# Two transformer blocks on one core: the first norm's gains, x and the first weights are loaded in another order and smaller pieces, and x is turned between the first products

## What is computed

```
h = rmsnorm(x, norm_mix_g[l])
proj = h @ w_in[l]            # (256, 2048) @ (2048, 4096)
```

## Time and profile before

| what | value |
|---|---|
| median of 3 runs | 2614.55 us (2613.58 to 2618.11) |
| the profiled execution, its own time | 2615.93 us |
| its span in the trace | 2613.8 us |
| TensorE busy in the span | 2590.8 us (99%) |
| VectorE, ScalarE busy | 1484.6 us (57%), 1105.7 us (42%) |
| first weight product starts | 13.41 us |
| granted clock of TensorE, mean | 0.996 of 2.4 GHz |

### The profile page before, as it was taken

How to read it: one execution, slowest core, us unless ns; L and a number is a source line. 1 busy time by engine, 2 the same in 40 slices (tenths; PEclk the granted TensorE clock), 3 DMA queues, 4 the chain that set the end, 5 groups by cost and what they waited for, 6 DMA issues and landing times.

```text
span 2613.8 us, 29869 instructions
## 1 busy us (share of the span) xinstructions
PE 2590.8 (99%) x13012; PEld 2188.5 (84%) x13012; DVE 1484.6 (57%) x1281; ACT 1105.7 (42%) x938; POOL 46.5 (2%) x58
## 2 busy tenths in 40 slices
PE   9999999999999999999999999999999999999998
PEld 7888888888888888888888887887888888888887
DVE  5465555544555455677678996534555544455444
ACT  5444454433444334455335444543354433344333
POOL 0000000000000000001001100000000000000000
PEclk9999999999999999999999999999999999999999
DMA  8544565666555655655334455553555555555553
GB/s 295 187 160 137 188 200 187 193 193 193 192 183 190 193 190 184 238 177 177 113 106 138 158 179 180 175 167 109 191 193 193 185 194 194 189 189 191 190 193 134
DMA packets 154753, 471.63 MB, mean 180 GB/s; under 512 B 7328, under 2 KB 7968, under 8 KB 153472
## 3 DMA queue, kind: packets, MB, share of 16 engines
q1 hardware_dynamic: 152208, 456.62, 53.2%
q0 software_dynamic: 1856, 11.54, 1.2%
q10 hardware_dynamic: 560, 1.57, 0.2%
HBM read 465.51 MB, written 4.19 MB: 180 GB/s over the span
## 4 chain that ended last, share of the span: by engine, by line
PE 96%; DVE 3%; ACT 1%; DMA 0%; issue 0%; POOLq 0%; SPq 0%; POOL 0%; ACTq 0%; DVEq 0%
PE ps L682 20%; PE ps L683 20%; PE ps L686 20%; PE ps L731 18%; PE ps L735 9%; PE ps L940 1%; DVE conv_out L1934 1%; PE ps L646 1%; PE ps L826 1%; DVE weights_lo L1714 1%; PE ps L1193 1%; PE ps L1209 1%; PE ps L1037 0%; PE ps L907 0%; PE ps L898 0%; PE ps L1111 0%
## 5 line engine op out<-in xcount | busy, mean ns | idle before, releaser
L1714 DVE TENSOR_TENSOR weights_lo<-weights_raw,weights_hi 128x2048 fp32r<-128x2048 f32 x431 | 986.8, 2290 | 926.8 <-ACT weights_hi L1277 926.8
L1277 ACT ACTIVATE weights_hi<-weights_raw 128x2048 fp32r<-128x2048 f32 x431 | 825.7, 1916 | 1149.1 <-PE ps L686 854.7
L682 PE MATMUL ps<-weights_hi,stationary 128*128 128x512 f32 x1408 | 559.3, 397 | 8.0 <-ACT stationary L1615 2.6
L683 PE MATMUL ps<-weights_lo,stationary 128*128 128x512 f32 x1408 | 549.9, 391 | 0.0
L731 PE MATMUL ps<-stationary,weights_hi 128*128 128x512 f32 x2048 | 547.9, 394 | 0.6 <-DVE residual L1747 0.6
L686 PE MATMUL ps<-weights_hi,stationary 128*128 128x512 f32 x1408 | 435.5, 391 | 0.0
L731 PEld LDWEIGHTS ps<-stationary,weights_hi 128*128 128x128 f32 x2048 | 354.6, 189 | 53.2 <-DVE residual L1747 0.9
L682 PE MATMUL ps<-weights_hi,hidden_hi 128*128 128x512 f32 x1016 | 395.3, 389 | 0.0
L683 PE MATMUL ps<-weights_lo,hidden_hi 128*128 128x512 f32 x1016 | 395.3, 389 | 0.0
L735 PEld LDWEIGHTS ps<-stationary,weights_lo 128*128 128x128 f32 x2048 | 305.5, 189 | 37.7
L682 PEld LDWEIGHTS ps<-weights_hi,stationary 128*128 128x128 f32 x1408 | 265.5, 189 | 65.0 <-issue 4.1
(11 more groups left out here) (320 smaller groups left out, 1106.9 us busy)
## 6 DMA issues: line engine op xcount, KB each, us to landing
weights_raw<-in_w SPq DMA_DIRECT2D x128, 1024.0 KB, 5.2
weights_raw<-in_w_in SPq DMA_DIRECT2D x79, 1024.0 KB, 5.2
weights_raw<-in_w_up SPq DMA_DIRECT2D x64, 1024.0 KB, 5.2
weights_raw<-in_w_down SPq DMA_DIRECT2D x64, 1024.0 KB, 5.4
weights_raw<-in_w_out SPq DMA_DIRECT2D x32, 1024.0 KB, 5.4
weights_raw<-in_wk SPq DMA_DIRECT2D x16, 1024.0 KB, 5.2
weights_raw<-in_wv SPq DMA_DIRECT2D x16, 1024.0 KB, 5.2
weights_raw<-in_wq SPq DMA_DIRECT2D x16, 1024.0 KB, 5.2
```

The source lines that it names most:

```text
L682: pe.matmul(o, xh, WHI[:, slot, j, c * BANK:(c + 1) * BANK], start=first and j == 0, stop=False)
L683: pe.matmul(o, xh, WLO[:, low, j, c * BANK:(c + 1) * BANK], start=False, stop=False)
L1277: act.activation(WHI[:, s % NSPLIT], RAW[:, s % NRAW], ACT.Copy).then_inc(hi_ready, 1)
L1714: dve.tensor_tensor(WLO[:, s % NRAW], RAW[:, s % NRAW], WHI[:, s % NSPLIT].bitcast(F32), ALU.subtract).then_inc(lo_ready, 1)
```

## The change

- `vectors` is loaded in two parts: the first block (64 KB, the gains of the norms) behind the identity, the other three (192 KB) behind weights 3. Both identity and gains count up `gains_landed`.
- `gains_turn` turns the one block; VectorE copies 128 columns and multiplies as before. The other three are turned by `vec_turn` ahead of step 6, into bank 7, and copied by VectorE after the low part of step 6. TensorE waits for this copy in the middle of step 7.
- x comes in pieces of tiles 0 and 1 (256 KB, ScalarE's queue), 2 and 3 (256 KB, between the halves of weights 0), 4 to 7 (512 KB, behind weights 1), and 8 to 15 (1024 KB, behind weights 2 and a wait of SyncE for the first piece).
- Ahead of step 0 only tiles 0 and 1 are turned and split, tiles 2 and 3 are turned after the first six products of step 0, and split behind the second half of weights 0. Two dummy products instead of four stand ahead of step 0.
- In steps 0 to 2 (`as_it_comes`) TensorE waits for each part just ahead of its first product, in the order high x high, low part of x x high, high part of x x low. The number of products is the same.

```
...
@@ -456,8 +456,8 @@
 
         @block.sync
         def _(sp):
-            sp.dma_start(VEC_RAW[:], vectors.rearrange("n r c -> r n c")).then_inc(vec_landed, 16)
-            sp.dma_start(SQ[:, 0, :], squares[:, 0, :]).then_inc(ident_landed, 16)
+            sp.dma_start(SQ[:, 0, :], squares[:, 0, :]).then_inc(gains_landed, 16)
+            sp.dma_start(VEC_RAW[:, 0, :], vectors[0]).then_inc(gains_landed, 16)
 
             def load(s, src):
 
@@ -469,9 +469,9 @@
                 for k in range(PS):
                     load(s0 + k, blocks(w)[(first + k) % PS, :, :, c0:c0 + COLS])
 
-            def load_x(n):
-                cols = slice(n * BANK, (n + 1) * BANK)
-                sp.dma_start(X[:, :, cols], x.rearrange("(t p) d -> p t d", p=P)[:, :, cols]).then_inc(x_landed[min(n, 2)], 16)
+            def load_x(n, first, end):
+                cols = slice(first * P, end * P)
+                sp.dma_start(X[:, :, cols], x.rearrange("(t p) d -> p t d", p=P)[:, :, cols]).then_inc(x_landed[n], 16)
 
             def load_up(s, src):
                 if s >= NRAW:
@@ -493,15 +493,19 @@
 
             first = blocks(w_in)[0, :, :, IN_COLS[0] * COLS:(IN_COLS[0] + 1) * COLS]
             sp.dma_start(RAW[:, 0, 0], first[:, 0]).then_inc(first_landed, 16)
+            load_x(1, 2, 4)
             sp.dma_start(RAW[:, 0, 1], first[:, 1]).then_inc(raw_landed[0], 16)
-            load_x(1)
             for n in range(4):
                 for k in range(PS):
                     if (n, k) != (0, 0):
                         load(S_IN + n * PS + k, blocks(w_in)[k, :, :, IN_COLS[n] * COLS:(IN_COLS[n] + 1) * COLS])
                     if (n, k) == (0, 1):
-                        load_x(2)
-                        load_x(3)
+                        load_x(2, 4, 8)
+                    elif (n, k) == (0, 2):
+                        sp.wait_ge(x_landed[0], 16)
+                        load_x(0, 8, KT)
+                    elif (n, k) == (0, 3):
+                        sp.dma_start(VEC_RAW[:, 1:, :], vectors[1:].rearrange("n r c -> r n c")).then_inc(vec_landed, 16)
                     elif (n, k) == (0, NRAW - 1):
                         sp.dma_start(SQ[:, 1:, :], squares[:, 1:, :]).then_inc(sq_landed, 16)
 
@@ -628,11 +632,14 @@
 
         @block.tensor
         def _(pe):
+            def gains_turn():
+                pe.wait_ge(gains_landed, 32)
+                pe.transpose(ps[:, 0, 0:P], VEC_RAW[:, 0, :], IDENT).then_inc(vec_turned, 1)
+
             def vec_turn():
                 pe.wait_ge(vec_landed, 16)
-                pe.wait_ge(ident_landed, 16)
-                for n in range(4):
-                    last = pe.transpose(ps[:, 0, n * P:(n + 1) * P], VEC_RAW[:, n, :], IDENT)
+                for n in range(1, 4):
+                    last = pe.transpose(ps[:, 7, n * P:(n + 1) * P], VEC_RAW[:, n, :], IDENT)
                 last.then_inc(vec_turned, 1)
 
             def turn8(src, half, group):
@@ -654,10 +661,7 @@
 
             def step(s, hi, lo, k, p, first, last, between=None):
 
-                if s == 0:
-                    pe.wait_ge(first_hi, 1)
-                    pe.wait_ge(first_lo, 1)
-                else:
+                if s >= NSPLIT:
                     pe.wait_ge(hi_ready, s + 1)
                     pe.wait_ge(lo_ready, s + 1)
                 slot, low, group = s % NSPLIT, s % NRAW, GROUPS[p]
@@ -671,10 +675,10 @@
                     if s == S_END - 1:
                         last_quarters(hi, lo, k, slot, low, group, t)
                         continue
+                    if s < NSPLIT:
+                        mm = as_it_comes(s, t)
+                        continue
                     for j in range(STEP):
-                        if (s, t, j) == (0, 0, 1):
-                            pe.wait_ge(hi_ready, 1)
-                            pe.wait_ge(lo_ready, 1)
                         xh = hi[:, k + j, t * P:(t + 1) * P]
                         xl = lo[:, k + j, t * P:(t + 1) * P]
                         for c in range(2):
@@ -689,6 +693,36 @@
                 if s < S_END - 1:
                     mm.then_inc(w_used, 1)
 
+            def as_it_comes(s, t):
+
+                for j in range(STEP):
+                    k = STEP * s + j
+                    xh = HHI[:, k, t * P:(t + 1) * P]
+                    xl = HLO[:, k, t * P:(t + 1) * P]
+                    if t == 0:
+                        pe.wait_ge(ht_hi, k + 1)
+                        if s == 0 and j == 0:
+                            pe.wait_ge(first_hi, 1)
+                        else:
+                            pe.wait_ge(hi_ready, s + 1)
+                    for c in range(2):
+                        pe.matmul(ps[:, 2 * t + c, :], xh, WHI[:, s, j, c * BANK:(c + 1) * BANK], start=k == 0, stop=False)
+                    if t == 0:
+                        pe.wait_ge(ht_lo, k + 1)
+                    for c in range(2):
+                        pe.matmul(ps[:, 2 * t + c, :], xl, WHI[:, s, j, c * BANK:(c + 1) * BANK], start=False, stop=False)
+                    if t == 0:
+                        if s == 0 and j == 0:
+                            pe.wait_ge(first_lo, 1)
+                        else:
+                            pe.wait_ge(lo_ready, s + 1)
+                    for c in range(2):
+                        mm = pe.matmul(ps[:, 2 * t + c, :], xh, WLO[:, s, j, c * BANK:(c + 1) * BANK], start=False, stop=False)
+                    if (s, t, j) == (0, 0, 0):
+                        pe.wait_ge(x_landed[1], 16)
+                        turn_tiles(residual, STEP, 2 * STEP, 1)
+                return mm
+
             def last_quarters(hi, lo, k, slot, low, group, t):
 
                 for c in range(2):
@@ -709,7 +743,7 @@
                         turn8(turn_second, 1, 1 - GROUPS[p])
                     if during:
                         during(k, 0)
-                    if h is not None:
+                    if h is not None and s0 + k >= NSPLIT:
                         stationary(h, STEP * (k + 1))
                     step(s0 + k, HHI, HLO, STEP * k, p, k == 0, k == PS - 1,
                          between=(lambda k=k: during(k, 1)) if during else None)
@@ -794,15 +828,20 @@
 
             pe.wait_ge(zeros_ready, 1)
             keep_busy(3)
-            vec_turn()
+            gains_turn()
             keep_busy(1)
 
             def during_wq_in(k, j):
                 if (k, j) == (1, 0):
-                    pe.wait_ge(x_landed[1], 16)
-                    turn_tiles(residual, 4, 8, 1)
+                    pe.wait_ge(x_landed[2], 16)
+                    turn_tiles(residual, 2 * STEP, 8, 1)
+                elif (k, j) == (6, 0):
+                    pe.wait_ge(ht_lo, KT * H_IN + KT)
+                    vec_turn()
+                elif (k, j) == (7, 1):
+                    pe.wait_ge(vec_ready, 2)
                 elif (k, j) == (2, 0):
-                    pe.wait_ge(x_landed[2], 32)
+                    pe.wait_ge(x_landed[0], 32)
                     pe.wait_ge(ht_lo, KT * H_IN + KT // 2)
                     turn8(residual, 1, 1)
 
@@ -814,9 +853,8 @@
                 pe.wait_ge(out1, p + 1)
 
             pe.wait_ge(x_landed[0], 16)
-            turn_tiles(residual, 0, 4, 1)
-            keep_busy(4)
-            pe.wait_ge(vec_ready, 1)
+            turn_tiles(residual, 0, STEP, 1)
+            keep_busy(2)
             gemm_pass(S_IN, P_IN, during_wq_in, H_IN)
 
             def turn_rows(src, group, done):
@@ -1363,25 +1401,26 @@
                     act.wait_ge(attended, h - 1)
                 act.activation(PT1[:, s, :], ps[:, 2 + s, 0:NS], ACT.Copy).then_inc(pt_ready, 1)
 
-            act.dma_start(X[:, :, 0:BANK], x.rearrange("(t p) d -> p t d", p=P)[:, :, 0:BANK]).then_inc(x_landed[0], 16)
+            act.dma_start(X[:, :, 0:T], x.rearrange("(t p) d -> p t d", p=P)[:, :, 0:T]).then_inc(x_landed[0], 16)
             act.wait_ge(halves_ready, 1)
             act.activation(table_warm[:], halves[:, 0:1], ACT.Copy)
             act.wait_ge(vec_ready, 1)
-            split_tiles(H_IN, lambda k: G_IN + k, 0, 4, 1)
+            split_tiles(H_IN, lambda k: G_IN + k, 0, STEP, 1)
             act.wait_ge(first_landed, 16)
             act.activation(WHI[:, 0, 0], RAW[:, 0, 0], ACT.Copy).then_inc(first_hi, 1)
             act.wait_ge(raw_landed[0], 16)
             act.activation(WHI[:, 0, 1], RAW[:, 0, 1], ACT.Copy).then_inc(hi_ready, 1)
+            split_tiles(H_IN, lambda k: G_IN + k, STEP, 2 * STEP, 1)
             for n in range(4):
                 for k in range(PS):
                     split_next(S_IN + n * PS + k)
                     if (n, k) == (0, 0):
-                        split_tiles(H_IN, lambda k: G_IN + k, 4, 8, 1)
+                        split_tiles(H_IN, lambda k: G_IN + k, 2 * STEP, 8, 1)
                     elif (n, k) == (0, 2):
                         split_turned(H_IN, lambda k: G_IN + k, 1, 1)
                     elif (n, k) == (0, 3):
```

(12 more changed lines are left out.)

2 lines of the change are left out of this document (1 added, 1 removed).

## The result

The changed kernel's median is 2611.64 us (20 runs, 2608.59 to 2614.69), that of the kernel before in the same comparison 2615.99 us (20 runs, 2612.76 to 2618.11). The medians are 4.35 us apart. Predicted were 2611.5 us in 2608.5 to 2615.0. In two later comparisons one run of the new version took 3914 and 4151 us, at a mean granted clock near 0.6, and is left out of the medians given for it.

A forecast was written before the change was run, and what follows sets the result against it. TensorE, busy 2590.8 of 2613.8 us, was taken as the bound, so only an earlier start helps: 4.5 us less 0.4, 0.44 and 0.33 is 3.3, taken as 3.0 for the clock; 2611.5 us predicted from 2614.55, range 2608.5 to 2615.0.

The forecast's parts named there:

- the working's 3.3: Whole start: 4.5 us gained at the first product, less 0.4, 0.44 and 0.33 us, gives 3.3 us.
- the clock term: Start: low clock from 8.0 to 11.4 us costs some 0.85 us, gain 2.45; otherwise 3.3; 3.0 taken.
- Transfers: First loads: 448 KB less ahead of the gains at 280 GB/s, 1.64 us; gains at 5.45, first half at 7.2 us.
- the first rival: Small pieces of x slow the queue: weights 1 at 14.2 us, gain 1.8 us, 2612.8 us; chance 0.17.
- From the gains to the first product: Start chain with two tiles on ScalarE and no wait for the low part: first product at 8.95 us, 4.5 gained.
- What goes back: Low part's wait 0.4 us, tiles 2 and 3 turned in step 0 0.44, step 6 transposes 0.33; second half nothing.
- the prediction's own early case: Gains at 4.0, first product at 7.5 us; second half holds tile 1; gain 4.1 us, 2610.5; chance 0.10.
- second way to step 1: Check on step 1's start: 20.00 us less 3.6 us gained is 16.4, against 16.1 by counting from step 0.
- The vectors' turn in step 6: VectorE waits for TensorE's step 6; low part of step 7 at 49.0, wanted at 51.2 us: costs nothing.
- First half not earlier: First half of weights 0 lands at 8.56 us as before: gain 2.5 us at full clock, 2612.3; chance 0.07.
- The slow case: Clock stays at 1.2 GHz while real products run; 2621 us at 20 us of it; chance 0.04, shared with one-by-one transfers.
- the gain at 27 us: Sign: products of step 2 at 23.4 to 24 us (27.22 before); prediction wrong if this gain isn't there at the end.

The follow-up runs named there:

- the four profiles: Profiles with the changed kernel's start as it is: its own two and those of experiment 8 and experiment 10; first pass taken out at 53.85 to 54.44 us.
- experiment 2: Changed kernel with tiles 0 to 3 of x in one piece again on ScalarE's queue: first pass taken out at 54.43 us, first product at 9.52.
- experiment 10: Wide sums and dummy products in the second block's waits, added to both kernels: 2611.41 us for the kernel before, 2607.62 us for the changed one.
- experiment 6: Changed kernel with one dummy product at the start and none of the three others: first pass taken out at 54.40 us (53.88 with the dummies).
- experiment 4: Kernel before with six more dummy products through TensorE's idle time from 4.1 to 7.2 us: first pass taken out at 56.60 us, 0.62 us less.
- experiment 8: Changed kernel with the layer norm's 16 sums of squares at 128 columns instead of 2: 2610.75 us, ratio to the kernel before 0.9983.

## Why the prediction was right

**The time.** 2611.5 predicted, 2611.64 measured. The mechanism is the predicted one, and the gain of 3.8 us without the spread (3.34 and 3.28 by the landmark in two pairs of profiles) stands beside the working's 3.3 and the chosen 3.0. The chosen value was low because of the clock term. That the times agree to 0.14 us is luck. The forecast took 3.05 us off a median of three runs, 2614.55; twenty runs have 2615.99, 1.4 us more, and the measured gain of 4.35 us is larger than the predicted one by 1.3. The two errors cancel, and both medians come from runs that spread over 5 to 6 us.

**Transfers.** The gains landed at 4.17 us (4.1 to 4.3 in the four profiles), near the lower bound of 4.0, not at 5.45. The rate of 280 GB/s, taken from the whole load, was the wrong measure for 128 KB at its very front. The first half came at 6.44 and not 7.2 in this execution, but at 7.8 and 7.5 in two others, so the 7.2 was fair. The other way, tiles 2 and 3 came at 8.3 (7.85 predicted), the second half at 9.51 (9.1; up to 10.2 in the four) and weights 1 at 12.1 (11.7): 0.4 us later than predicted, not the 2.5 of the first rival. Counted from the first half's landing in this execution it is 1.2 us. From 5 to 6.5 us the four profiles moved 168 to 213 GB/s, the three with the start of the kernel before 317 to 331, and experiment 2, with tiles 0 to 3 of x in one piece, 268. So the change's loads are slow there; which of its pieces makes it isn't shown.

**From the gains to the first product.** 8.11 us against 8.95, a gain of 5.3 us at this point and not 4.5. The copy of 128 columns took 0.29 us (0.28 assumed), and ScalarE's two tiles and half weights went as counted (1.93 us, 1.95 assumed). Of the 1.3 us by which the gains came earlier 0.45 were lost on the way to ScalarE's start, because the dummy product and the transposes of x weren't at full pace (4.22 to 6.18 us; in experiment 10 the same way took 1.31 us).

**What goes back.** The wait for the low part came, and was a little smaller: 1.17 us from the first product to the fifth, where the prediction had 1.25 (8.95 to 10.2). What it had wrong is the second half of weights 0, which it called free. Step 0's tile 1 begins at 10.74, 1.46 us after the fifth product and not 0.9, because TensorE waits for the high part; and tile 1 takes 4.52 us and not 4.1, because TensorE waits for the low part (11.90). Together that is 0.9 to 1.0 us. So step 0 took 7.15 us from its first product and not 6.25, which cancels the 0.8 us: two errors of one size, and that the sum came out is in part luck. It isn't luck alone, since the prediction's own early case says that the second half would hold tile 1 if the start came earlier. Step 0 ended at 15.26 us (15.2 predicted), step 1 began at 16.05 (16.1), and the turn ahead of step 2 at 21.59 (21.7), because from there on all goes by the tensor engine's own pace. This was the part to get right, and it was read from the engine's 46.6 us without idle time. For its second way to step 1 the prediction took 20.00 from the chain; the first product of step 1 is at 19.76 in the timeline of the kernel before, and 3.6 less is 16.2.

**The later steps.** The low part of weights 1 was ready at 16.34 and wanted at 17.0: cover of 0.7 us as predicted, no wait. The vectors' turn in step 6: VectorE waited 6.91 us, copied in 0.56, and had the low part of step 7 ready at 48.4, wanted at about 51; TensorE didn't wait:

```profile
45.68 0.56 DVE L1900 COPY vectors<-ps 128x384 f32<-128x384 f32 x1 [6.91 <-PE ps L642]
46.16 4.48 DVE L1753 TENSOR_TENSOR weights_lo<-weights_raw,weights_hi 128x2048 fp32r<-128x2048 f32 x2
```

The three transposes cost what was counted: the gain is 3.71 us at the turn ahead of step 2 (25.30 to 21.59) and 3.34 at the end of the pass.

**The clock.** Two predicted cases, 2.45 if low from 8.0 to 11.4 and 3.3 if not. It was not: the first two products took 0.70 us, where they take 1.19 at the low clock. Experiment 6 gives the low case 0.4 to 0.5 us and not 0.85. (The "four dummy products taken out" are two products, of two instructions each.) The prediction saw the low clock of the kernel before and took it as a possible loss after the change only. It also delayed the kernel before, by 0.6 us and more by experiment 4; a part of this was in the sum without a name, as four transposes at the fast pace.

**The rivals.** Small pieces: true in kind, 0.4 us. Earlier transfers: true at the front, without use behind it, since the second half didn't come earlier. First half not earlier: false, 6.4 to 7.8 against 8.56. The slow case: no products at the low pace beyond 12 us at the start in any profile. What no rival named is that the low clock at 1420 to 1610 us, far from the change, moves single executions by up to 5 us. Two of the prediction's signs came out otherwise. TensorE's busy time is 0.6 us longer, not a few tenths shorter. And the gain at 27 us isn't there at the end of the first pair of profiles (1.7 us of 3.7), which was to mean a wrong prediction; with the low clock equal, in the second pair, 3.2 us are there.

**Left open.** The landmark at the end of the pass differs between executions of one kernel, by when the first loads land (the means are 57.6 and 54.1, 3.5 us apart); so the 3.3 us of the first pairs and the 3.8 us of run 10 aren't told apart. How much of the 4.35 us in the first comparison is chance in the low clock can't be said from the times; run 10 puts it at some 0.5 us. Why the clock falls behind the same wait in one execution and not in another wasn't tried, and the wide sums and the two fills were never timed apart except for experiment 8.

## What to carry to other kernels

At the start of a kernel the bytes ahead of the first gate count: here 192 KB more of vectors turned the gains 1 us later. Load what the first instruction needs as a piece of its own, ask for each operand just ahead of its first use (about 1 us here by itself), and then look which landing is now the last, because the gain ends there: here the second half of weights 0 took back 0.9 us. Read a wait of the tensor engine from the starts of its products and from its weight loads, since the ends are modelled. When a change is worth less than the spread, find the spread in the profiles first: a fixed landmark in both traces gave 3.3 us from one pair, and filling two waits and widening 32 thin products took 4 to 5 us off both kernels and cut the spread from 5 or 6 us to under 1. Where two profiles differ far away from the edit, compare the granted clock there before looking for a cause in the edit.

## What the runs showed of the hardware

A busy tensor engine can lose its clock: during the 32 products with two columns it counts as busy without pause, and yet the granted clock fell to 1.2 GHz at 1592.8 us in the first profile of the changed kernel, so that they took 4.8 us (from 1590.64 to 1595.48) and not the 3.63 of a profile in which it stayed up. It fell during these products or within 1.5 us behind them in eight of the ten profiles that have them, and in none of the four in which they have 128 columns; of these only experiment 8 has the waits as they were. In the three profiles with wide sums and both waits filled it was not low between 1372 and 1912 us. The Trainium skill (TensorE: Matmul & The Clock Gate, Part 1) says that activity releases the throttle. The trace agrees for the kernel as a whole, with a mean granted clock of 0.996 at 99% busy; this case adds that the clock also fell while the trace has the engine busy.

The record of the granted clock is not complete at the start of an execution. In the second profile of the kernel before it says 1.00 throughout the first 13 us, while eight transposes took 1.91 us, the pace of the low clock (1.92 in the first profile, where it says 0.50, and 1.04 in experiment 4); experiment 6 has the same, with its first products at 1.19 us:

```profile
8.68 1.91 PE L646 MATMUL ps<-squares,residual 128*128 128x128 f32 x8
```

and the windows of that profile:

```profile
8.50:9.00 0.50, 0.50 (x3) 0.32 (x2) 0.43 (x2) 0.00 (x0) 0.00 (x0) 1.00 1.05 410
9.50:10.00 0.50, 0.50 (x5) 0.50 (x4) 0.00 (x0) 0.16 (x1) 0.00 (x0) 1.00 1.08 434
```

For the first microseconds the pace of equal instructions is the better witness.
